# Fourteen of twenty-four modulation rows formed by VectorE beside the PEER feed-forward, forty early up tiles, sixteen gate rows kept, and a reordered opening, mixer stage and mixture prelude

## The reference, cut to what matters

```python
# first block: mixers, then PEER
z = x @ w_in + b_in                       # v_a, u_a, q, k, v_b, g_a, g_b
v = layer_norm(gelu(v_a), ln_g, ln_b)     # then spatial gating, attention, projections
...
q = (h @ w_q);  s = einsum(q, sub_keys);  top 16 of 128 twice, top 16 of the 256 sums
gates = softmax(best_s)                   # 8 heads x 16 experts a token, of 128 x 128 experts
hid = gelu(u_tab[ec] . xc)                # up
y = (gates * hid) . v_tab[ec]             # down
# third block: modulation from the condition c
cond = silu(c)
mod = cond @ ada_w[layer] + ada_b[layer]  # two layers x 6144 values
...
y = moe_swiglu(hn, router_w, wg, wu, wd)  # 8 experts, 2 a token
```

## Time and profile before

| | |
|---|---|
| median of 3 runs | 3210.19 us (3208.39 to 3212.88) |
| profiled execution | 3213.16 us |
| its span | 3211.4 us |
| granted TensorE clock, mean | 0.977 |
| PE busy | 3030.2 us (94%) |
| DVE busy | 2136.6 us (67%) |
| ACT busy | 1576.2 us (49%) |
| DMA | 647.64 MB, mean 202 GB/s |

### The profile page before, as it was taken

How to read it: one execution, slowest core, us unless ns; L and a number is a source line. 1 busy time by engine, 2 the same in 40 slices (tenths; PEclk the granted TensorE clock), 3 DMA queues, 4 the chain that set the end, 5 groups by cost and what they waited for, 6 DMA issues and landing times. The chain is left out here.

```text
span 3211.4 us, 49257 instructions
## 1 busy us (share of the span) xinstructions
PE 3030.2 (94%) x19808; PEld 2621.5 (82%) x19808; DVE 2136.6 (67%) x3333; ACT 1576.2 (49%) x2500; POOL 96.4 (3%) x132
## 2 busy tenths in 40 slices
PE   7999999899999999979999899999998789999997
PEld 6897876679999998858978699768987679999997
DVE  5456498766666666376665666756545768888887
ACT  3443313444444444264443544544345358778875
POOL 0000000000000000200000000000000100000000
PEclk9999999999999999989998999999999989999999
DMA  6444488865666554404533254324542058899895
GB/s 263 164 166 161 158 339 354 328 220 206 223 214 209 201 197 171 148 19 155 192 147 131 90 192 165 138 79 159 194 177 105 1 204 334 334 335 329 328 338 198
DMA packets 76688, 647.64 MB, mean 202 GB/s; under 512 B 6088, under 2 KB 31176, under 8 KB 34016
## 3 DMA queue, kind: packets, MB, share of 16 engines
q1 hardware_dynamic: 49440, 620.05, 51.7%
q10 hardware_dynamic: 27072, 25.17, 2.5%
HBM read 631.56 MB, written 13.63 MB: 201 GB/s over the span
## 5 line engine op out<-in xcount | busy, mean ns | idle before, releaser
L1187 PE MATMUL ps<-x_hi,up_hi 128*128 128x256 f32 x1632 | 459.4, 282 | 2.3 <-DVE up_lo L1278 2.0
L1191 PE MATMUL ps<-x_hi,up_lo 128*128 128x256 f32 x1632 | 458.4, 281 | 0.0
L1190 PE MATMUL ps<-x_lo,up_hi 128*128 128x256 f32 x1632 | 458.3, 281 | 0.0
L346 DVE TENSOR_TENSOR weight_lo<-ring,weight_hi 128x1024 fp32r<-128x1024 f32 x236 | 289.6, 1239 | 252.8 <-ACT weight_hi L339 245.2
L1283 DVE TENSOR_TENSOR down_lo<-ring,down_hi 128x1024 fp32r<-128x1024 f32 x182 | 222.9, 1225 | 166.1 <-ACT down_hi L1242 166.1
L339 ACT ACTIVATE weight_hi<-ring 128x1024 fp32r<-128x1024 f32 x236 | 245.3, 1053 | 176.7 <-PE ps L516 107.9
L1187 PEld LDWEIGHTS ps<-x_hi,up_hi 128*128 128x128 f32 x1632 | 309.7, 190 | 10.9 <-DVE up_lo L1278 3.0
L1190 PEld LDWEIGHTS ps<-x_lo,up_hi 128*128 128x128 f32 x1632 | 309.9, 190 | 6.7
L1191 PEld LDWEIGHTS ps<-x_hi,up_lo 128*128 128x128 f32 x1632 | 309.8, 190 | 0.0
L1242 ACT ACTIVATE down_hi<-ring 128x1024 fp32r<-128x1024 f32 x182 | 193.4, 1063 | 231.7 <-PE ps L1212 231.7
L494 PE MATMUL ps<-x_hi,weight_hi 128*128 128x256 f32 x1024 | 292.4, 286 | 6.6 <-DVE weight_lo L346 5.7
(11 more groups left out here) (542 smaller groups left out, 6445.2 us busy)
## 6 DMA issues: line engine op xcount, KB each, us to landing
ring<-in_stream SPq DMA_DIRECT2D x181, 2048.0 KB, 7.7
ring<-in_experts SPq DMA_DIRECT2D x121, 1536.0 KB, 8.6
ring<-in_stream SPq DMA_DIRECT2D x22, 1536.0 KB, 6.3
gates<-kept_gates ACTq DMA_DIRECT2D x12, 1024.0 KB, 8.8
kept_gates<-away_first ACTq DMA_DIRECT2D x8, 768.0 KB, 10.7
kept_gates<-away_last ACTq DMA_DIRECT2D x8, 768.0 KB, 9.3
params_mix<-in_mix SPq DMA_DIRECT2D x1, 3072.0 KB, 22.0
params_ln<-in_ln SPq DMA_DIRECT2D x2, 1024.0 KB, 5.7
```

Source lines behind the costliest of these rows:

```text
L346: dve.tensor_tensor(self.place(self.lo, b), self.raw(b), self.place(self.hi, b), ALU.subtract).then_inc(self.split, 1)
L1187: last = pe.matmul(out, hi[:, o:o + P], x_hi[:, k, :], start=(k == 0), stop=False)
L1190: pe.matmul(out, hi[:, o:o + P], x_lo[:, k, :], start=False, stop=False)
L1191: last = pe.matmul(out, lo[:, o:o + P], x_hi[:, k, :], start=False, stop=(k == DK - 1))
```

## The change

- `EARLY` goes from 32 to 40: 40 tiles have their up product in the search and the spreading, and the feed-forward runs 88 tiles. `SEARCH_CHUNKS` goes from 6 `u` and 12 `a` to 7 `u` and 2 `a`; `SPREAD_CHUNKS` from 2 `u` and 12 `a` to 3 `u` and 8 `a`. PE makes 10 rows (`ROWS_ON_PE`).
- The other 14 rows travel as chunks of the feed-forward, one after every three tile chunks. DVE forms each in eight parts of 128 x 512 (multiply by a column of the condition and add), two a tile during four of every six tiles, one after `up_lo` and one after `down_lo`. Its last part frees the ring slot (`row_used`). PE sums the 128 partitions of four rows at a time with a product by ones into bank 2, and DVE adds the result to `mod` at the end. The loops of this stage are written out.
- `KEPT` goes from 32 to 16: a store of gates holds 112 rows (896 KB in place of 768 KB), and groups are reloaded from the third on, during early down too.
- The opening loads chunk 0 in four quarters, each with a semaphore, and ACT's first copies wait for their quarter. DVE splits weight blocks 4 to 6 before it waits for `params_mix`, and one weight block after each step of the layer norm.
- In the mixture prelude ACT turns the columns before it splits weights.

```diff
-KEPT = 32
+KEPT = 16
-EARLY = 32
-SEARCH_CHUNKS = "uaauaauaauaauaauaa"
-SPREAD_CHUNKS = "aauaaaaauaaaaa"
+EARLY = 40
+SEARCH_CHUNKS = "uuauuuauu"
+SPREAD_CHUNKS = "auaauaauaaa"
+FORWARD_CHUNKS = "ff" + 14 * "afff"
+ROWS_ON_PE = (SEARCH_CHUNKS + SPREAD_CHUNKS).count("a")
+LATE_ROWS = [n for n, kind in enumerate(FORWARD_CHUNKS) if kind == "a"]
+ROW_TILES = 6
...
+    def feed_quarters(self, sp, early):
+        self.early = early + [self.loaded[0]]
+        for q, landed in enumerate(self.early):
+            o = slice(q * D, q * D + D)
+            sp.dma_start(self.slot(0)[:, o], self.dram[0, :, o]).then_inc(landed, 16)
+        self.asked = 1
...
+                if c - RING in self.rows:
+                    sp.wait_ge(self.row_used, self.rows.index(c - RING) + 1)
+                elif c >= RING:
+                    sp.wait_ge(self.used, self.freed_before(c - RING) + 1)
...
-            if self.blocks[b][2] == 0:
+            if self.blocks[b][0] == 0:
+                act.wait_ge(self.stream.early[b], 16)
+            elif self.blocks[b][2] == 0:
                 self.stream.wait(act, self.blocks[b][0])
...
             dve.tensor_scalar(spare[:], moments[:, :, 1], LN_EPS, None, ALU.add).then_inc(var_ready, 1)
+            between(0)
             for t in range(TT):
                 last = dve.scalar_tensor_tensor(y[:, t, :], y[:, t, :], moments[:, t, 0:1], g, ALU.subtract, ALU.mult)
             step(last)
+            between(1)
...
                 last = dve.scalar_tensor_tensor(out[:, t, :], y[:, t, :], rstd[:, t:t + 1], b, ALU.mult, ALU.add)
+                between(2 + t)
...
                         if b % 2:
                             weights.low(dve, b // 2 + 1)
+                    weights.low(dve, 7)
                     dve.wait_ge(params_loaded, 16)
...
+                    def sum_rows(which):
+                        pe.wait_ge(stream.row_used, which[-1] + 1)
+                        for r in which:
+                            band, n = r % 4 * BAND, ROWS_ON_PE + r
+                            last = pe.matmul(ps[band:band + BAND, 2, :], rows[1][:, BAND - 1 - n:2 * BAND - 1 - n], rows[2][:, r % 4, :],
+                                             start=(r < 4), stop=(r + 4 >= len(LATE_ROWS)), skip_group_check=True)
+                        last.then_inc(rows_summed, 1)
...
+                        due = rows_from(j)
                         if i is not None or j + 2 < tiles:
                             split_up(j + 2, i)
+                        for r in due:
+                            row_part(r, 2 * (j - ROW_TILES * r - 1))
                         if i is not None or j + 1 < tiles:
                             split_down(j + 1, i)
+                        for r in due:
+                            row_part(r, 2 * (j - ROW_TILES * r - 1) + 1)
+
+                    def row_part(r, k):
+                        chunk = first + LATE_ROWS[r]
+                        to, w = rows[2][:, r % 4, :], stream.slot(chunk)[:, k * WIDE:k * WIDE + WIDE]
+                        if k == 0:
+                            stream.wait(dve, chunk)
+                            if r >= 4:
+                                dve.wait_ge(rows_summed, r // 4)
+                            dve.tensor_scalar(to, w, rows[0](k), None, ALU.mult).then_inc(row_step, 1)
+                            return
+                        dve.wait_ge(row_step, (DK - 1) * r + k)
+                        ins = dve.scalar_tensor_tensor(to, w, rows[0](k), to, ALU.mult, ALU.add)
+                        ins.then_inc(row_step if k < DK - 1 else stream.row_used, 1)
...
+                    if rows is not None:
+                        dve.wait_ge(rows_summed, (len(LATE_ROWS) + 3) // 4)
+                        dve.tensor_tensor(mod[:], mod[:], ps[:, 2, :], ALU.add)
...
+                    norm.columns(act)
                     up_high_of(0, 0)
                     up_high_of(0, 1)
-                    norm.columns(act)
```

More of the change, by code:

```diff
@@ L124, in _chunk_layout @@
         out.append((early if kind == "u" else rows).pop(0))
-    assert not rows and not early
     for j in range(0, EARLY, 4):
         out.append(np.concatenate(list(v[j:j + 4]), 1))
-    for j in range(EARLY, KEYS, 2):
-        out.append(np.concatenate([u[j], v[j], u[j + 1], v[j + 1]], 1))
+    pairs = [np.concatenate([u[j], v[j], u[j + 1], v[j + 1]], 1) for j in range(EARLY, KEYS, 2)]
+    for kind in FORWARD_CHUNKS:
+        out.append((pairs if kind == "f" else rows).pop(0))
+    assert not rows and not early and not pairs
     def mlp(up, down):
@@ L260, in __init__ @@
         self.pending = False
+        self.early = []
     def release(self, ins):
@@ L269, in slot, with freed_before @@
         return self.ring[:, c % RING, :]
+    def feed_quarters(self, sp, early):
[4 more added lines that the diff above has]
+        self.asked = 1
+    def freed_before(self, c):
+        return c - sum(1 for r in self.rows if r < c)
     def feed(self, sp, n):
@@ L281, in feed @@
             w = self.widths[c]
-            if c >= RING and turns >= 2:
+            if c >= RING and turns >= 2 and not any(c - RING <= r < c + turns * RING for r in self.rows):
                 with sp.Fori(0, turns) as i:
                     for s in range(RING):
-                        sp.wait_ge(self.used, i * RING + (c + s - RING + 1))
+                        sp.wait_ge(self.used, i * RING + (self.freed_before(c + s - RING) + 1))
                         src = self.dram[bass.ds(i * RING + (c + s), 1), :, 0:w].rearrange("a p n -> (a p) n")
@@ L1149, in raw, with rows_from, rows_until @@
                     o = j % per_chunk * size
-                    return stream.slot(first + j // per_chunk)[:, o:o + size]
+                    return stream.slot(first + of_tiles[j // per_chunk])[:, o:o + size]
+                def rows_from(j):
+                    return [r for r in range(len(LATE_ROWS)) if ROW_TILES * r + 1 <= j < ROW_TILES * r + 5] if rows is not None else []
+                def rows_until(j):
+                    r = (j - 5) // ROW_TILES
+                    if rows is None or j % ROW_TILES != 5 or not (r % 4 == 3 or r == len(LATE_ROWS) - 1):
+                        return []
+                    return list(range(r // 4 * 4, r + 1))
                 def run(eng, step, n, times=1):
                     span = turn * times
-                    turns = max((n - head) // span, 0)
+                    turns = max((n - head) // span, 0) if rows is None else 0
                     for j in range(min(head, n)):
@@ L1268, in _ @@
                     split_down(0)
-                    run(act, step, tiles - 2, times=KEPT // turn if kind == "peer" else 1)
+                    run(act, step, tiles - 2)
                     for j in range(tiles - 2, tiles):
@@ L1324, in _ @@
                     split_down(0)
-                    run(dve, step, tiles - 2, times={"moe": EXPERTS, "peer": KEPT}.get(kind, turn) // turn)
+                    run(dve, step, tiles - 2, times={"moe": EXPERTS}.get(kind, turn) // turn)
                     for j in range(tiles - 2, tiles):
                         step(j)
+                    if rows is not None:
+                        dve.wait_ge(rows_summed, (len(LATE_ROWS) + 3) // 4)
+                        dve.tensor_tensor(mod[:], mod[:], ps[:, 2, :], ALU.add)
                 if norm is not None:
@@ L1593, in peer @@
                 buf_2, p = params("ln2", dense)
-                feed_forward("peer", KEYS - EARLY, ACT.Gelu, x_parts, scale_by=gates, starts=False, work=work, ahead=(buf_2[:], d["ln2"]))
+                row_sums = sbuf("row_sums", [P, 4, WIDE], mem=dense)
+                feed_forward("peer", KEYS - EARLY, ACT.Gelu, x_parts, scale_by=gates, starts=False, work=work, ahead=(buf_2[:], d["ln2"]),
+                             rows=(lambda k: cond_at[:, k, BAND - 1:BAND], one_at, row_sums))
             with signals("bias_loaded", "mean_ready", "squared", "var_ready", "rstd_ready", "weighed", "normed", "dve_step") as (
@@ L1805, in split_down, with load @@
                         act.activation(down_hi[:, j % 2, :], raw(j), ACT.Copy).then_inc(down_hi_ready, 1)
[L1807 to L1810 removed]
+                    def load(group):
+                        act.wait_ge(full_ready, GROUP * (group + 1))
+                        load_gates(act, gates, group % (KEPT // GROUP), group)
                     split_down(0)
@@ L1827, in scale @@
                         tokens = lambda ap: ap.rearrange("p (b m) -> p b m", m=SPAN)
-                        dve.tensor_tensor(tokens(full[:, j % 2, :]), tokens(acted_of(j)), gates[:, j // GROUP, :, j % GROUP, :],
+                        group = j // GROUP
+                        slot = group % (KEPT // GROUP)
+                        if j % GROUP == 0 and j >= KEPT:
+                            dve.wait_ge(gates_loaded[slot], 16 * (group // (KEPT // GROUP)))
```

(1 more changed line is left out.)

62 lines of the change are left out of this document (35 added, 27 removed).

## The result

The kernel after takes **3174.47 us** (median of 4 runs, 3173.95 to 3175.27) against 3209.41 for the kernel before (3208.39 to 3212.88, 4 runs): ratio 0.9889, 95% interval 0.9872 to 0.9907. The forecast was 3171.2 us with a range of 3158 to 3188. The profiled execution took 3173.95 us, 39.2 less than the one of before (3213.16); the medians are 34.9 apart. The sum of the prediction was -39.0.

What follows compares the result with a forecast made beforehand. PE was taken as the bound (94% busy), losing time at gaps, with transfers costing time in the spreading. Terms -14.1 - 1.9 + 23.4 - 44.4 + 3.5 - 5.5 = -39.0 us gave a median of 3171.2 us, range 3158 to 3188.

Steps and rivals of the forecast that it cites:

- The sum: Whole kernel: all terms together give -39.0 us against the profiled 3213.16, so 3174.2, and a median of 3171.2.
- Opening, -14.1: Opening and mixers: earlier first copy -3.8, two PE gaps -3.3 and -3.7, their lower clock -1.7 and -1.6 us.
- Search, +1.4: Search: the first exponential stands behind 14 gelus instead of 12, so DVE resumes 1.4 us later.
- Spreading: Spreading: the 6.9 us stall goes; pieces 10 to 28 take 60.4 us, so the last three rows begin at 598.3.
- The end of the spreading: Spreading to early down: 8.1 MB at 381 GB/s delay the last gate store to 619.6, PE's start to 623.2.
- the rival's case: End of spreading: stores do not bind, early down starts with PE's own end at 614; 3162 us, chance 0.17.
- The rule of turns: Spreading's stores: even turns would land a 0.77 MB store in 4 us; the trace, at 10.9, does not bear them out.
- Early down, +23.4: Early down: eight more early tiles at 2.93 us each add 23.4 us.
- Feed-forward, -44.4 + 3.5: Feed-forward: eight fewer tiles at 5.55 us save 44.4 us; PE's 28 float32 sum instructions add 3.5.
- Row parts, 0: Feed-forward: parts near 0.69 us fit DVE's two gaps a tile (1.07 and 0.91 us), costing 0.
- the slower rival: Feed-forward: DVE becomes the bound above 0.99 us a part; 1.34 eats the 39.0, 1.5 gives 3228 us; chance 0.03.
- Mixture, -5.5: Mixture prelude: columns begin 4.3 us earlier, plus 1.2 us as PE has no long gap before the router product.

Runs made afterwards that it cites:

- e12: Kernel after with only the low parts between the layer norm's steps undone: 3181.44 us, ratio 0.9913 to the kernel before.
- e1: Kernel after with all three edits of the opening and mixers undone (quarters, early low part, layer norm): 3186.94 us, ratio 0.9927 to before.
- e9: Kernel after with the spreading asking for one chunk instead of three ahead of early down: 3168.78 us, ratio 0.9864 to before.
- e6: Kernel after with ACT's wait for the gate stores moved to the eighth early down tile: 3165.05 us, ratio 0.9853 to before.
- e3: Kernel after with 32 early tiles instead of 40, late rows kept on DVE: 3190.23 us, ratio 0.9933 to before.
- e4: Kernel after with all 24 rows made by PE, the 14 late ones in the search: 3217.12 us, ratio 1.0021 to before.
- e5: Kernel after with seven of each late row's eight parts repeated into a spare buffer: 3175.36 us, ratio 0.9886 to before.
- e10: Kernel after with two extra 448-column multiply-adds ahead of seven of each late row's eight parts: 3202.06 us, ratio 0.9977 to before.
- e2: Kernel after with ACT again making the first two high parts ahead of the mixture's columns: 3180.36 us, ratio 0.9904 to before.
- e8: Kernel after with the gate-store wait at the eighth early down tile and the first exponential behind 13 gelus: 3164.23 us, ratio 0.9863 to before.
- e11: Kernel after with only the first chunk's quarters undone, so it comes as one transfer: 3177.15 us, ratio 0.9901 to before.
- e7: Kernel after with the search's first exponential behind 13 gelus instead of 14: 3172.89 us, ratio 0.9875 to before.

## Why the prediction was right, step by step

- **The sum.** -39.0 forecast, -39.2 between the two profiled executions, -34.9 between the medians. That the first two agree to 0.2 us is luck: by the table the terms are off by 0.7 to 2.2 us each and cancel, and the stages that nothing touches moved by +1.7. The forecast time is 3.3 us too low because I took the 3.0 us by which before's profiled execution lay above its median off the result too; after's lies 0.5 us *below* its median. One execution's distance from its median is no property of the kernel.
- **Opening, -14.1.** Measured -13.4 in the trace, 14.1 by undoing it. Start 3.8 (3.2 in the timeline, 3.7 undone), layer norm 3.7 + 1.6 (3.7 + 1.5 in e12's rows, 6.3 in the length), blocks 4 to 6 3.3 + 1.7 (4.1 by difference, 2.15 + 1.7 in e1's rows). That the clock's share belongs to the gaps is shown by e1 and e12.
- **Search, +1.4.** Measured -0.7, but the two executions are not alike at the start of the stage. PE has a gap of 2.5 us there, and behind it before's has a granted clock of 0.66 over 5 us and after's one of 1.00: ACT takes the first early tile 5.5 us after PE's first product in before and 3.8 in after. e9, e10 and e12, which leave the search alone, are like before. Windows of after and of e9, then e9's timeline at the first exponential:
```profile
374.70:379.70 5.00, 5.00 (x23) 4.43 (x24) 4.96 (x35) 1.63 (x2) 0.00 (x0) 1.00 0.82 329
374.70:379.70 5.00, 4.98 (x15) 4.11 (x16) 4.97 (x35) 1.27 (x1) 0.00 (x0) 0.66 0.87 342
```
```profile
429.22 0.29 DVE L1623 TENSOR_REDUCE gate_sum<-found 128x8 f32<-128x128 f32 x1 [4.08 <-ACT found L1637]
```
In e9 DVE waits 4.08 us (4.1 forecast) and resumes 1.4 us later in the stage than in before, and the stage is 1.0 us longer than before's. Like with like, mechanism and size held. The -0.7 is the luck of which execution was profiled: six other executions with this search unedited have after's length to 0.1 us and three have 1.7 us more.
- **Spreading.** The last batch was to begin at 598.3 in before's time. It began at 585.17 + 13.4 = 598.6.
- **The end of the spreading: the term that failed.** I let the last store land when all 8.1 MB had landed, at 619.6, and PE begin at 623.2. It landed at 604.37 (617.8 in before's time), 4.3 us ahead of the last chunk (608.64), and PE began at 605.46 (618.9). A store does not queue behind the whole burst. The 1.6 us for the clock was there, but behind the first product. Nor is it the rival's case (PE's own end, 614): that is what e6 reaches.
- **The rule of turns.** The Trainium skill (DMA: Bandwidth & Descriptors, "Queues, rings and completion order") has each DMA engine serve its queues in turn, a packet from each. I had read it as equal bytes. The rows of after's DMA view give 5.23 MB / 351 = 14.9 KB a packet for the ring and 0.92 MB / 145 = 6.3 KB for the store. A turn each gives the store 6.3 / 21.2 = 0.30 of the bytes; at the 411 GB/s of that view, an estimate by that rule, 0.92 MB take 7.5 us. The store of after, issued at 592.53, falls into two parts. DMA views of 592.5 to 596.1 and of 596.1 to 603.9 us, the second queue being absent from the first:
```profile
q1 hardware_dynamic: 101, 1.39, 99.2%
```
```profile
q1 hardware_dynamic: 159, 2.34, 71.7%
q10 hardware_dynamic: 144, 0.92, 28.0%
```
For 3.6 us no packet of it moves. Then 144 packets of it go beside 159 of the ring, 0.28 of the bytes, in 7.8 us: for this part the trace agrees with the rule. In e9 the same two parts are 593 to 595 and 595 to 599.4 us:
```profile
q1 hardware_dynamic: 51, 0.84, 97.8%
```
```profile
q10 hardware_dynamic: 144, 0.92, 50.2%
q1 hardware_dynamic: 16, 0.00, 0.2%
```
It waits 2.0 us and then moves alone, so e9 says nothing of sharing. In e3 its first packet comes 0.8 us after the issue. So a store asked for beside chunks pays twice, by a wait ahead of its first packet (0.8, 2.0 and 3.6 us with none, one and three chunks asked for) and by sharing. What sets the length of that wait stays open.
- **Early down, +23.4.** Measured +24.7 from the first product, and the 1.3 more are the lower clock behind the gap. But e3 shows that the eight tiles cost 29.4 in all, since the gap of 5.2 us came with them. In the forecast that gap stood in the spreading's term (before had one of 1.27 there).
- **Feed-forward, -44.4 + 3.5.** 88 tiles at 5.55 us. The sums cost 4.8 us (e4 without them: 491.0), 28 instructions at 0.17 instead of 0.114 each.
- **Row parts, 0.** Right in the result, and wrong in the bound. I wrote that two parts fit into a tile "up to 0.99 us each" and that DVE becomes the bound above. e5 has four parts in a tile, 2.6 us from start to start, and costs nothing. By the two conditions of e10 two parts may take 5.55 + 2.6/4 - 3.48 = 2.7 us together, 1.36 each (estimated, from e5 and e10). At the slower rival's break-even of 1.34 us a part DVE would be 4 x (3.48 + 2.68 - 5.55) = 2.4 us behind and need 31.6 us for six tiles: by this estimate it would have cost nothing, which no run shows. The step that was wrong is that the gaps of one tile are all the room there is.
- **Mixture, -5.5.** -6.5 in the trace, 6.3 undone, both against one of the shortest of the twelve executions that have this stage as it is, which reach 2.9 us more. The wait held; the 1.2 us for what follows it is not told from the scatter.
- **The other stages, 0.** +1.7 together. The largest is the stage from 1306 to 1327 us, 21.0 instead of 18.3 long. It took 18.3 us in e2, e4 and e8, 20.0 in e1, e3, e5, e6, e9, e11 and e12, and 20.9 in e7 and e10, though nothing in it is edited. It follows the granted clock over the stage, which is 0.99 in before, 1.00 in e2, e4 and e8, 0.91 or 0.92 in the seven of 20.0 us, and 0.87 or 0.88 in after, e7 and e10.

## What to carry to other kernels

Whether extra work fits beside a full engine is a matter of the mean over the period and of how far the helper may fall behind, not of the gaps of one iteration. A stage's difference between two executions is read only after its granted clock has been compared: here one gap of 2.5 us was worth 1.7 us in some executions and nothing in others. When work is moved into the last free slots of a stage, look at which transfers are now released beside the stage's last store, and put the wait for that store where its data is read. Short work with large operands (a row: 1.8 us of PE, 4.9 us of transfer) belongs where transfers have room, whichever engine does it.

## What the runs showed of the hardware

- DVE instructions overlap: a part on 128 x 512 float32 lasts 0.745 us, but in e5 they follow each other at 0.66 (starts at 937.86, 938.52, 939.18). A sum of durations overstates DVE's load, here by 0.085 us an instruction.
- The same store of 0.92 MB took 3.5, 6.3 and 11.8 us with none, one and three chunks of 2 MB asked for beside it, of which 0.8, 2.0 and 3.6 us passed before its first packet. Once it moved beside the ring, the two queues went about packet for packet (144 and 159).
- Two switches of ACT's tables, 1.28 us each, stand around the exponential between gelus (425.80 and 427.42 in after), and the first of them was on the path of the search.
- A gap of 3.7 us on PE cost about 1.5 us more at the lower clock in e12, and the waits of e4 made the same 448 products 12 us longer.
- Behind the same gap of 2.5 us ahead of the search's first product the clock fell to the lower level (1.2 GHz) in before, e4, e9, e10 and e12 and stayed at the higher one (2.4 GHz) in after and the other eight runs.
